# Merge stage of a hybrid decoder layer: block products in sevens, output projection in a phase of its own

## What is computed

```python
branch = jnp.einsum('bskw,kwd->bskd', ys, branch_w)          # 4 branches, 256 -> 1024
gates = jax.nn.sigmoid(xn @ merge_gate_w + merge_gate_b).reshape(bn, s, N_BRANCH, d)   # 1024 -> 4096
merged = jnp.sum(gates * branch, axis=2)
return merged @ w_out                                         # 1024 -> 1024
```

## Time and profile before

| | |
|---|---|
| median of 3 runs | 2485.73 us |
| profiled execution, its span | 2490.9 us |
| TensorE busy | 2344.6 us, 94% |
| VectorE, ScalarE, GpSimd busy | 55%, 44%, 27% |
| DMA | 517.42 MB, mean 208 GB/s |
| first merge matmul, last merge operation | 459.18 us, 1571.95 us |

### The profile page before, as it was taken

One profiled execution on the slowest core, in us unless ns is written; L12 is line 12 of the kernel. 1 busy time (PEld: TensorE's weight loads), 2 busy tenths in 40 slices (PEclk: granted clock), 3 DMA queues, 4 the chain that ended last, 5 costly groups with the idle time before them and its releaser, 6 DMA issues. The chain is left out here.

```text
span 2490.9 us, 33940 instructions
## 1 busy us (share of the span) xinstructions
PE 2344.6 (94%) x11340; PEld 1842.1 (74%) x11341; DVE 1374.7 (55%) x2038; ACT 1107.2 (44%) x1410; POOL 675.7 (27%) x516
## 2 busy tenths in 40 slices
PE   6999989999999999999999999499999999999991
PEld 5777768788888888888888887377667776677771
DVE  7697767644443444444443444656555655557565
ACT  4534333233333333333333332367556665567663
POOL 3831101100000000000000000277555756558771
PEclk9999999999999999999999999699999999999995
DMA  7964846443463335433453323398778888789987
GB/s 216 354 245 161 317 155 203 125 129 96 131 215 126 99 114 188 151 120 95 152 192 93 95 85 126 137 336 318 269 260 290 300 293 288 261 306 365 326 289 287
DMA packets 314109, 517.42 MB, mean 208 GB/s; under 512 B 35420, under 2 KB 213856, under 8 KB 297632
## 3 DMA queue, kind: packets, MB, share of 16 engines
q1 hardware_dynamic: 297520, 458.44, 52.4%
q0 software_dynamic: 16496, 57.74, 9.3%
HBM read 431.17 MB, written 84.94 MB: 207 GB/s over the span
## 5 line engine op out<-in xcount | busy, mean ns | idle before, releaser
L1555 PE MATMUL mrgps<-xn_hi,w_hi 128*128 128x512 f32 x1016 | 397.0, 391 | 0.0
L1555 PE MATMUL mrgps<-xn_lo,w_hi 128*128 128x512 f32 x1016 | 395.4, 389 | 0.0
L1555 PE MATMUL mrgps<-xn_hi,w_lo 128*128 128x512 f32 x1016 | 395.4, 389 | 0.0
L2088 POOL TENSOR_TENSOR w_lo<-w_raw,w_hi 128x1024 fp32r<-128x1024 f32 x128 | 343.6, 2835 | 0.0
L2252 PE MATMUL exps<-w_hi,x_room 128*128 128x512 f32 x1024 | 331.5, 400 | 3.5 <-DVEq L2423 3.0
L1476 ACT ACTIVATE gt<-mrgps,mb 128x512 f32<-128x512 f32 x128 | 88.3, 690 | 507.1 <-PE mrgps L1555 500.5
L1827 POOL MEMSET x_ident<- 128x128 f32 x1 | 0.2, 200 | 1110.8 <-POOLq L1271 1110.8
L2083 DVE TENSOR_TENSOR w_lo<-w_raw,w_hi 128x2048 fp32r<-128x2048 f32 x127 | 285.4, 2306 | 0.0
L1693 DVE SCALAR_TENSOR_TENSOR tmp<-gt,mrgps 128x512 f32<-128x512 f32 x96 | 66.0, 687 | 384.9 <-PE mrgps L1555 384.9
L2073 ACT ACTIVATE w_hi<-w_raw 128x2048 fp32r<-128x2048 f32 x128 | 239.1, 1921 | 9.1 <-DMA w_raw<-in_expert_w_dram 9.0
L2252 PEld LDWEIGHTS exps<-w_hi,x_room 128*128 128x128 f32 x1024 | 193.4, 189 | 63.4 <-issue 16.9
(11 more groups left out here) (449 smaller groups left out, 4150.2 us busy)
## 6 DMA issues: line engine op xcount, KB each, us to landing
w_raw<-in_expert_w_dram SPq DMA_DIRECT2D x192, 1024.0 KB, 8.8
w_raw<-in_merge_gate_w_dram SPq DMA_DIRECT2D x128, 512.0 KB, 4.0
win_hi<-w_in_parts SPq DMA_DIRECT2D x42, 512.0 KB, 4.1
win_lo<-w_in_parts SPq DMA_DIRECT2D x42, 512.0 KB, 5.6
w_raw<-in_branch_w_dram SPq DMA_DIRECT2D x128, 128.0 KB, 4.1
wout<-in_w_out_dram SPq DMA_DIRECT2D x64, 256.0 KB, 4.7
w_raw<-in_x_dram SPq DMA_DIRECT2D x16, 512.0 KB, 7.8
branch_rows<-in_x_dram SPq DMA_DIRECT2D x16, 512.0 KB, 5.8
```

Of the source, the lines that this page charges most:

```text
L1555: last = pe.matmul(bank[:], w[:, u % 2, kk], x, start=(kk == w_tiles[0] and j == 0), stop=(kk == w_tiles[-1] and j == 2))
L2088: eng.tensor_tensor(self.lo2[:, f], self.raw2[:, f], self.hi2[:, f].bitcast(F32), ALU.subtract).then_inc(self.split2, 1)
```

## The change

Gate products and w_out are block products. The weight (1024 by 256) and the moving operand (1024 by 1024) are each cut in 2 by 2 blocks, so that a block product is 4 contraction tiles by 3 = 12 matmuls of 128x128 by 512. The plain form has 8 of them for four output corners (FOUR, for the first two steps only); the new form has 7 (FAST), from sums and differences of blocks, whose results are combined afterwards.

- A step q replaces four units: two output tiles (a pair) by two token chunks, for one branch. Steps 0 to 31 make gates (two pairs of token chunks, 16 steps each), each with 24 branch matmuls; steps 32 to 39 make w_out for 256 tokens each and both halves of the output.
- Per step GpSimd makes the weight sums s1 to s4 of the raw weights (weight_sums); ScalarE and VectorE split seven items into a ring of five slots (part_high, part_low). There is one room for raw weights: the load of the next step waits for the split of item 22 of this one (load_raw).
- The combined x blocks t1 to t4 are made in steps 0 and 1 from chunks 3 and 2 (x_sums, x_combine), for the second pair of chunks in steps 3 to 10 into DRAM (stage), for w_out in steps 18 to 25. At steps 15 and 31 the seven blocks in SBUF are loaded anew (refill), each as soon as its product has been issued for the last time.
- Results: the first product is copied by ScalarE (first_copy), VectorE adds u2, z and three corners (second, third, corner), then tanh, multiplication and addition for each corner (tanh, gate).
- The merged rows are stored in DRAM (store_merged) and come back as the raw weights of the w_out steps. Norm, transposes and router of a step's two tiles stand inside the next step; those of the last step follow it.
- The branch rows of the last chunk are stored by the mixer and loaded again, two tiles for each step (load_ys). The mixer loads only the first step's weights.
- The gate bias is loaded as the fifth DMA on SP, and VectorE scales it before anything else; norm and router parameters are loaded between the gate phase and the w_out phase.

The parts of the diff that the prediction speaks of:

```diff
+            store(1, CH - 1, yb_full, pl)
+            store(3, CH - 1, yd_full, lg)
+            store(0, CH - 1, ya_full, ya)
             sp.wait_ge(xT_out, 64 * (CH - 1))
             for b in range(NBR):
-                sp.wait_ge(ys_out[b], 16 * (CH - 1))
+                sp.wait_ge(ys_out[b], 16 * (CH - (b == 2)))
...
+    FAST = (("11", "11", "a"), ("s2", "t2", "b"), ("12", "21", "a"), ("s1", "t1", "c"), ("s3", "t3", "d"), ("s4", "22", "c"), ("22", "t4", "d"))
+    FOUR = (("11", "11", "a"), ("12", "21", "a"), ("21", "11", "d"), ("22", "21", "d"),
+            ("11", "12", "c"), ("12", "22", "c"), ("21", "12", "b"), ("22", "22", "b"))
...
+            def load_raw(q):
+                if q >= 1:
+                    low.reached(sp, (q - 1, "22"))
...
+            load_ys(0)
+            load_x2(0)
+            sp.dma_start(mb[:], io["merge_gate_b"][0].rearrange("(k d p) -> p k d", k=NBR, p=P), allow_slow_non_contiguous=True).then_inc(par_in, 16)
...
+                if last:
+                    refill(q, 0)
+                if q and (q - 1) % NBR == NBR - 1:
+                    for c in corners[kind(q - 1)]:
+                        store_merged(q - 1, c)
+                load_raw(q + 1)
+                if last:
+                    for i in (1, 2, 3):
+                        refill(q, i)
+                here = FIRST[m] <= q < FIRST[m] + STEPS
+                if here and m == 1:
+                    for b in staged[m][0:3]:
+                        store_stage(v, b)
+                if q + 1 < NA:
+                    load_ys(q + 1)
+                if here:
+                    for b in staged[m][-4:]:
+                        store_stage(v, b)
+                if FIRST[m] <= q + 1 < FIRST[m] + STEPS:
+                    load_stage(v + 1)
+                if last:
+                    for i in (4, 5, 6):
+                        refill(q, i)
+            for c in corners["gate"]:
+                store_merged(NA - 1, c)
+            load_rows(NA)
+            for c in corners["gate"]:
+                sp.wait_ge(acc_out[c], 16 * KD)
+            sp.dma_start(g2, io["norm2_g"][0:1].partition_broadcast(P)).then_inc(rpar_in, 16)
...
+            for q in range(NA, NQ):
+                if q > NA:
+                    store_h(q - 1, 0)
+                    store_h(q - 1, 1)
+                if q + 1 < NQ:
+                    load_raw(q + 1)
+                if q > NA:
+                    store_xn(q - 1, 0)
+                    store_xn(q - 1, 1)
+                    load_rows(q)
...
+            for q in range(PLAIN, NA):
+                for i in range(5):
+                    product(q, i)
+                branches(q)
+                for i in (5, 6):
+                    product(q, i)
...
+            dve.wait_ge(par_in, 16)
             dve.tensor_scalar(mb[:], mb[:], 0.5, None, ALU.mult).then_inc(half_b, 1)
...
+            for q in range(PLAIN, NA):
+                m = q // PER
+                v = q - FIRST[m] + m * STEPS
+                here = FIRST[m] <= q < FIRST[m] + STEPS
+                part_low(q, "s4")
+                if here and m == 1:
+                    stage_low(v, staged[m][0:3])
+                second(q)
+                part_low(q, "22")
+                third(q)
+                if here:
+                    stage_low(v, staged[m][-4:])
+                corner(q, "22")
+                for i in ("11", "s2", "12"):
+                    part_low(q + 1, i)
+                gate(q, "11")
+                if q + 1 < NA:
+                    wb_low(q + 1)
+                gate(q, "22")
+                corner(q, "12")
+                gate(q, "12")
+                part_low(q + 1, "s1")
+                if q + 1 < NA:
+                    rows_low(q + 1)
+                part_low(q + 1, "s3")
+                corner(q, "21")
+                gate(q, "21")
+            dve.wait_ge(rpar_in, 16 * 5)
+            for q in range(NA, NQ):
+                r = q - NA
+                if r:
+                    norms(r - 1)
+                part_low(q, "s4")
+                second(q)
+                part_low(q, "22")
+                third(q)
+                residual(q, "11")
+                if q + 1 < NQ:
+                    part_low(q + 1, "11")
+                    part_low(q + 1, "s2")
+                corner(q, "22")
+                residual(q, "22")
```

More of the change, by code:

```diff
@@ L1662, in _ @@
+            r = NQ - 1 - NA
+            turn(r, 0)
+            rout(r, 0)
+            turn(r, 1)
+            back(r, 0)
+            rout(r, 1)
+            back(r, 1)
         @block.vector
```

1097 lines of the change are left out of this document (658 added, 439 removed).

## The result

| | before | after |
|---|---|---|
| median | 2485.02 us | 2585.26 us |
| lowest to highest run | 2483.79 to 2494.85 | 2580.95 to 2588.63 |
| profiled execution, its span | 2490.9 us | 2581.4 us |
| last merge operation | 1571.95 us | 1666.04 us |
| from there to the end | 919.0 us | 915.4 us |

The ratio is 1.0392, 95% interval 1.037 to 1.0415. The changed kernel is slower, as forecast, but by 100 us and not by 20. In the two profiled executions the merge stage ends 94.1 us later and the rest takes 3.6 us less, so the 90.5 us of span lie in the merge.

A forecast was written before the change was run, and what follows sets the result against it. The merge stage was taken to be bound by the number of matmuls. Added terms of +123 us against -103.4 saved gave +20, so 2506 us from a median of 2485.7; own range 2480 to 2540, whole range 2420 to 2545.

The forecast's parts named there:

- Saving: Steps 2 to 39 make seven products of 12 matmuls in place of eight: 456 matmuls fewer, -103.4 us.
- Start: First merge matmul waits for the gate bias, and the barrier for the store of ya: +12 us (8 to 16).
- Gate steps: TensorE waits 0.7 us at the third product in 23 gate steps: +16 us (0 to 50).
- a chain of 8.9 us: Gate steps, sixth product's end to next step's third product: 8.9 us with handoffs, while TensorE has 8.2 us of work.
- the first staging: Staging of x blocks in steps 3 to 10: sums of engine work below 24.5 us a step, so no cost.
- Staging of w_out: Steps 18 to 25: seven blocks through four rooms, three splits wait for stores of the same step: +20 us (5 to 30).
- Exchange at step 16: Branch rows of step 16 and raw weights of step 17 land behind replaced blocks: +18 us (8 to 28).
- Step 32: VectorE waits for norm and router parameters before its first split, delaying the seventh product: +32 us (15 to 38).
- w_out steps: Steps 33 to 38: norm chain and late copies of the turned tile, 3.9 us of wait per step: +28 us (10 to 40).
- rival 4: Short idle of each gate step also halves the clock, 2.4 us in 23 steps: +55, 2561 us; chance 0.03.
- Rival 1: GpSimd's four sums hold VectorE up 2.4 us in each of 30 steps: +72, 2578 us; chance 0.05.
- my own case: Whole kernel: the forecast of 2506 us, its own range 2480 to 2540; chance 0.48.

The follow-up runs named there:

- e12: Changed kernel with all edits of order as in e11, weight sums on VectorE except in steps 19 to 26 and the w_out steps; median 2510.7 us, ratio 1.009.
- e1: Changed kernel with the gate bias as first DMA on SP's queue, not fifth; ratio to before 1.038, last merge operation 1660.4 us.
- e3: Changed kernel without staging of combined blocks, exchanges loading as many bytes from elsewhere; last merge operation 1615.4 us, 50.6 below the changed kernel.
- e14: Changed kernel with weight sums on 8 of 128 columns, each behind three GpSimd memsets of 320 columns; median 2495 us, last merge operation 1623.6 us.
- e16: e12 with the split of item 22 ahead of u2 and the staged blocks; median 2484.9 us, ratio to before 0.9981.
- e15: Changed kernel with weight sums on 8 of 128 columns, each behind two GpSimd additions of 160 columns; last merge operation 1632.5 us, ratio 1.004.
- e9: Changed kernel with ScalarE's copy of the next step's first product ahead of the tanh of corner 21; ratio to before 1.038, last merge operation 1664.2 us.
- e11: Changed kernel with all edits of order together, weight sums left on GpSimd; median 2551.7 us, ratio to before 1.025.

## Why the prediction was right or wrong

**Saving.** Right: 456 matmuls, 0.227 us apart where nothing waits. TensorE's count shows it, and e12's steps of 24.2 us show that the seven products run at full rate.

**Start.** Right in size (12, measured 13.3) and cause (13.37 us of wait for the bias). e1 shows that it was not worth its size: 14 us earlier at the first matmul were 5.7 at the end, or less, because VectorE and the x blocks were next.

**Gate steps.** The mechanism was named (P2 behind ScalarE's copy, behind VectorE's corner), the term was mis-sized: 12 us outside of steps 15 to 26, measured 66.5. The step that failed is the list of prices. I took 0.69 us for every 512-wide operation on VectorE and 1.2 for GpSimd's, both from rows where the other engine did nothing next to it, and a chain of 8.9 us against 8.2 has no room for error. Beside GpSimd's operations a weight split takes 1.3 to 1.4 us, and a sum of GpSimd up to 1.7. I also put the first staging at 0, since its mean load fits in 24.5 us; e3 gives it 12.5.

**Staging of w_out.** Right sign, 24 against 41.8, and a reason that the runs don't bear out. The wait for rooms is in the trace (57 us on ScalarE), and its removal gives 3.3, with the weight splits pushed beside the sums. What the runs do show is 15.6 us for staged splits of 0.82 us in place of 0.42 beside the sums (e14), and that the loop by the raw room holds these steps up once the orders are mended (e16). What the wait for the rooms is worth by itself stays open.

**Exchange at step 16.** Right: 18, measured 16.7. **Step 32.** 32, measured 27.5; the wait for the parameters is there, released at 1417.53, and SP issued them in 4.3 us and not in 8.5. But it hid a second wait, for the rows of x, so undoing it gave 7.5. The prediction never asked what would be late next if this wait were gone. **w_out steps.** 28, measured 33.8, the router's wait of 3.7 to 4.2 us as described.

**Clock.** I counted slow matmuls in four terms and ruled them out in the gate steps (rival 4, idle of 0.7 us). With idles of 2.3 to 5.6 us they came there too. They are 51 of the 194 us, the stage's share of the lower level.

**Rival 1 was nearly right.** It gave 2578 for 2585, by 2.4 us of VectorE held up in each step, and I gave it 0.05. What made me do so is the comparison 2306 against 2288 ns, "with GpSimd's splits beside them". They were not beside them. In the trace of before, expert stage, VectorE's splits and GpSimd's:

```profile
1819.02 8.88 DVE L2083 TENSOR_TENSOR w_lo<-w_raw,w_hi 128x2048 fp32r<-128x2048 f32 x4
...
1798.73 2.35 POOL L2088 TENSOR_TENSOR w_lo<-w_raw,w_hi 128x1024 fp32r<-128x1024 f32 x1
...
1806.93 5.28 POOL L2088 TENSOR_TENSOR w_lo<-w_raw,w_hi 128x1024 fp32r<-128x1024 f32 x2
...
1826.65 3.47 POOL L2088 TENSOR_TENSOR w_lo<-w_raw,w_hi 128x1024 fp32r<-128x1024 f32 x1
```

Four splits on VectorE from 1819.0 to 1827.9; GpSimd's are before and after. Taken from the timeline of the whole expert stage, only 35 of the 285 us of VectorE's splits have a GpSimd split beside them. They touch 28 times. 25 times VectorE's split runs first, as at 1826.65: it keeps its 2.28 us, and GpSimd's takes 3.51 us on average. (The 2.35 us above are of a second split, right behind another. GpSimd's splits that begin such a run with no VectorE split beside them, 24 of them, take 2.93.) Three times GpSimd's runs first, and there it is VectorE's that is long:

```profile
2288.17 7.66 POOL L2088 TENSOR_TENSOR w_lo<-w_raw,w_hi 128x1024 fp32r<-128x1024 f32 x3
...
2294.63 3.35 DVE L2083 TENSOR_TENSOR w_lo<-w_raw,w_hi 128x2048 fp32r<-128x2048 f32 x1
```

It takes 3.35 us in place of 2.28. The evidence for rival 1 was in these rows, on both sides, and means over 127 and 128 instructions hid it. That rival 1's time is so near is in part luck: in its account the sums only hold VectorE up, and the runs give 42 us for VectorE and GpSimd shut out by each other, 20 for the lateness of the sums, and staging its part.

**Chances.** Of the 0.48 for my own case none had room for a price that is wrong in all steps alike. A chain that is 0.7 us too long for its cover, and 23 times, deserved an upper bound from doubled operations: 17.8 us of chain in place of 8.9, 9.6 us over its cover, 23 times. That is 220 us, and a range that ended at 2545 left all of it out.

What stays open: the 33.5 us between e15 and the changed kernel, and how the 27 us of steps 0 to 3 divide. There e9 took step 2 from 32.0 to 25.8 us and e12 to 24.5, but later steps gave it back in e9.

## What to carry to other kernels

Before the mean of a group serves as proof that two engines don't disturb each other, look in the timeline whether they ran at the same time; then price each operation of a chain beside its neighbour and not alone. Work put on an idle GpSimd is not free where VectorE works on tiles in SBUF: with the same orders, most of the sums moved to VectorE gave 41 us by the medians and 51 by the profiles (e11 against e12). And where a wait is the longest in its queue, ask what is late behind it before the change is credited with it: 57 us of store waits gave 3 when other splits took their place beside the sums, 14 us at the start gave 6 at most, and 25 us of parameters 7.5.

## What the runs showed of the hardware

- A GpSimd addition and a VectorE operation with two SBUF inputs exclude each other per instruction, both ways: a 512-wide split goes from 0.69 to 1.3 to 1.4 us on average, up to 1.8 beside 512-wide sums and 2.87 beside the 1024-wide ones of the staging; a 256-wide split from 0.42 to 0.82; a 512-wide sum from 1.29 to between 1.4 and 1.7. The one that starts second is the longer (before: VectorE 3.35 in place of 2.28 us, GpSimd 3.51 in place of 2.93). VectorE operations with a PSUM input stay at 0.68 to 0.69, and GpSimd memsets disturb nothing (1493 ns for the 1280-wide split beside them and without).
- The cost of this to a tightly ordered kernel is larger than the busy time shows: 42 us in the merge, where ten additions of 160 columns a step at another moment cost 7.7.
- Waits of TensorE up to 2.1 us left its clock at 2.4 GHz; behind 13 of the 14 of 2.27 us and more in steps 3 to 31, matmuls came 0.35 to 0.44 us apart on average (0.23 behind one of 2.80 us).
